# One kernel, four edits: the scan's block matrix built by overlapping reads from DRAM, the modulation split over two stages, and weights loaded in another order

## What is computed

```python
def reference(x, c, ...):
    cond = jax.nn.silu(c)
    for i in range(DEPTH):
        mod = cond @ ada_w[i] + ada_b[i]
        sh1, sc1, g1, sh2, sc2, g2 = jnp.split(mod, 6, axis=-1)
        hn = modulate(rmsnorm(x, norm1_g[i]), sh1, sc1)
        ...  # out = s5_mixer(hn, ...) in layer 0, short_conv_mixer in layer 1
        x = x + (1 + g1)[:, None, :] * out
        hn = modulate(rmsnorm(x, norm2_g[i]), sh2, sc2)
        x = x + (1 + g2)[:, None, :] * hier_moe(hn, ...)
    return rmsnorm(x, final_g)

def s5_mixer(h, w_in, ...):
    u = (h @ w_in).astype(f32)
    ...  # st[t] = a * st[t-1] + b u[t] for each group, in chunks
    ...  # y = Re(c st) + d_skip * u
    val, gate = jnp.split(gelu(y) @ w_glu, 2, axis=-1)
    return val * jax.nn.sigmoid(gate)
```

## Time and profile before

| | us |
|---|---|
| median of 3 runs | 7016.55 (7015.04 to 7017.35) |
| the profiled execution | 7015.28 |
| its span | 7013.7 |
| PE busy | 6407.3 (91%) |
| DVE busy | 3326.9 (47%) |
| ACT busy | 2051.1 (29%) |
| POOL busy | 1448.3 (21%) |

### The profile page before, as it was taken

The page is one execution under the profiler, slowest core; times in us unless marked ns, Lnnn a source line. Parts: engine busy times, 40 slices in busy tenths (PEclk is TensorE's granted clock), DMA queues, the critical chain, the costliest instruction groups (busy, mean ns, idle before and its releaser), DMA issues. The chain is left out here.

```text
span 7013.7 us, 90561 instructions
## 1 busy us (share of the span) xinstructions
PE 6407.3 (91%) x30729; PEld 5236.7 (75%) x30730; DVE 3326.9 (47%) x4885; ACT 2051.1 (29%) x3301; POOL 1448.3 (21%) x1250
## 2 busy tenths in 40 slices
PE   6997888799996999999997999998998699999994
PEld 1876667588884788888886888886776588888883
DVE  4445666343336555555643422222545654466554
ACT  1112443222221343343433500000111243344434
POOL 0001222488002232222321000000000322232222
PEclk8998999899998999999998999999998899999997
DMA  6221111444222676676754544433334365677766
GB/s 205 66 87 46 48 50 48 158 142 144 85 84 79 199 223 178 186 215 200 225 157 149 194 178 166 148 135 137 133 131 141 117 189 167 191 217 237 222 200 244
DMA packets 528270, 1073.08 MB, mean 153 GB/s; under 512 B 59550, under 2 KB 137374, under 8 KB 527146
## 3 DMA queue, kind: packets, MB, share of 16 engines
q1 hardware_dynamic: 425364, 805.88, 33.6%
q0 software_dynamic: 69888, 249.12, 14.1%
q10 hardware_dynamic: 32920, 16.80, 0.8%
HBM read 816.33 MB, written 255.38 MB: 153 GB/s over the span
## 5 line engine op out<-in xcount | busy, mean ns | idle before, releaser
L127 PE MATMUL conv_p<-conv_x_lo,conv_w_hi 128*128 128x512 f32 x1536 | 601.1, 391 | 0.0
L128 PE MATMUL conv_p<-conv_x_hi,conv_w_lo 128*128 128x512 f32 x1536 | 598.5, 390 | 0.0
L129 PE MATMUL conv_p<-conv_x_hi,conv_w_hi 128*128 128x512 f32 x1536 | 598.3, 390 | 0.0
L1758 DVE SCALAR_TENSOR_TENSOR m_o<-m_pO,m_weight_of,m_gate 128x512 f32<-128x512 f32 x320 | 237.0, 746 | 726.6 <-POOLq L1398 376.6
L1725 DVE TENSOR_TENSOR m_w_lo<-m_w_raw,m_w_hi 128x1024 fp32r<-128x1024 f32 x496 | 577.6, 1214 | 0.0
L1533 ACT ACTIVATE m_xT_hi<-m_pX 128x512 fp32r<-128x512 f32 x320 | 191.6, 599 | 1151.9 <-PE m_pB L129 994.2
L127 PE MATMUL m_pA<-m_w_lo,m_xT_hi 128*128 128x512 f32 x1280 | 517.0, 404 | 5.7 <-DVE m_xT_lo L1736 5.7
L1474 PE MATMUL m_pO<-m_w_lo,m_hT_hi 128*128 128x512 f32 x1280 | 512.8, 401 | 0.5 <-ACT m_hT_hi L1538 0.5
L1521 ACT ACTIVATE m_w_hi<-m_w_raw 128x1024 fp32r<-128x1024 f32 x512 | 505.3, 1053 | 0.0
L129 PE MATMUL m_pA<-m_w_hi,m_xT_hi 128*128 128x512 f32 x1280 | 503.0, 393 | 0.0
L128 PE MATMUL m_pA<-m_w_hi,m_xT_lo 128*128 128x512 f32 x1280 | 499.9, 391 | 0.0
(11 more groups left out here) (354 smaller groups left out, 12702.6 us busy)
## 6 DMA issues: line engine op xcount, KB each, us to landing
m_w_raw<-in_moe_w_dram SPq DMA_DIRECT2D x384, 1024.0 KB, 7.3
conv_x_hi<-hT_hi SPq DMA_DIRECT2D x24, 2048.0 KB, 9.3
conv_x_lo<-hT_lo SPq DMA_DIRECT2D x24, 2048.0 KB, 13.9
mod_w<-in_ada_w_dram SPq DMA_DIRECT2D x12, 2048.0 KB, 7.8
glu_ada<-in_ada_w_dram POOLq DMA_DIRECT2D x96, 256.0 KB, 3.1
a_x<-in_x_dram SPq DMA_DIRECT2D x32, 512.0 KB, 3.5
u<-a_stage POOLq DMA_DIRECT2D x4, 4096.0 KB, 19.2
s_u<-u SPq DMA_DIRECT2D x64, 256.0 KB, 2.6
```

Source lines behind the costliest of these rows:

```text
L127: pe.matmul(out, lh, rl, start=start, stop=False)
L128: pe.matmul(out, ll, rh, start=False, stop=False)
L129: return pe.matmul(out, lh, rh, start=False, stop=stop)
L1758: dve.scalar_tensor_tensor(out=ob[:, n, :], in0=pO[:, n, :], scalar=wslot[:, bass.ds(tile_, 1)], in1=gate2[:, n, :], op0=ALU.mult, op1=ALU ...
```

## The change

1. **Tables.** `Modulation` computes only 4 of the 12 chunks (`sh1`, `sc1`), with a buffer for each; SP issues them after the small loads. Its first loads go out on ACT, and POOL adds the biases and stores the row. `skip` is loaded by four DMAs on POOL into four blocks of 16 partitions; DVE and PE no longer wait for it.
2. **Input.** The other 8 chunks are summed on POOL (`PartialSums`, the code that "glu" had, with three slots in place of four), two chunks ahead of each of the four stores of `u`. After the last tile SP reads the partial sums (2 MB), PE adds up their partitions in eight products, ACT copies them and stores them to `mod`. The three constants are issued by POOL, `w` is loaded and split in pieces of 256 rows by 512 columns, bank by bank, and the times in a block are stored in reverse.
3. **Scan.** The four groups of a batch share one PSUM bank `pK`: each group adds one product of `z[g]` (its b in 16 of 128 columns) with `O`. Once a batch `out_k` adds the skip and copies it out; SP stores it to DRAM behind a pad of zeros, waits, and loads `R` of each group by a read whose eight row blocks overlap, each 16 elements further. `inside` waits for these loads.
4. **Projection.** `src` goes out first, then the weights in pieces by bank (1 MB in "glu", 0.5 MB in "cout"). POOL issues the eight constants when the sixth piece has landed, and DVE folds them after the weights are split.

```diff
     def loads(self, sp):
-        with sp.Fori(1, self.ROUNDS) as i:
-            self.load(sp, i, 0)
-            self.load(sp, i, 1)
-
-    def store(self, sp):
-        sp.wait_ge(self.added, 2 * self.ROUNDS)
-        sp.dma_start(self.dst, self.row[:]).then_inc(self.st, 16)
-        sp.wait_ge(self.st, 16)
+        for q in range(self.CHUNKS):
+            sp.dma_start(self.w[q][:], self.w_view[:, :, bass.ts(q, HALF)]).then_inc(self.w_ld[q], 16)
...
+    def products(self, pe):
         pe.wait_ge(self.cond_ready, 1)
-
-    def products(self, pe, a, b):
-
-        with pe.Fori(a, b) as i:
-            for s in range(2):
-                pe.wait_ge(self.w_ld[s], 16 * i + 16)
-                pe.wait_ge(self.out[s], i + 1)
-                for k in range(KD):
-                    last = pe.matmul(self.ps[s][0:1, :], self.cond_sb[:, 1, k:k + 1], self.w[s][:, k, :],
-                                     start=k == 0, stop=k == KD - 1)
-                last.then_inc(self.mm[s], 1)
+        for q in range(self.CHUNKS):
+            pe.wait_ge(self.w_ld[q], 16)
+            if q >= 2:
+                pe.wait_ge(self.out, q - 1)
+            for k in range(KD):
+                last = pe.matmul(self.ps[q % 2][0:1, :], self.cond_sb[:, 1, k:k + 1], self.w[q][:, k, :],
+                                 start=k == 0, stop=k == KD - 1)
+            last.then_inc(self.mm, 1)
...
+    def biases(self, pool):
+        pool.wait_ge(self.b_ld, 16)
+        for q in range(self.CHUNKS):
+            pool.wait_ge(self.out, q + 1)
+            c = bass.ts(q, HALF)
+            pool.tensor_tensor(self.row[0:1, c], self.row[0:1, c], self.bias[0:1, c], ALU.add).then_inc(self.added, 1)
+        pool.wait_ge(self.added, self.CHUNKS)
+        pool.dma_start(self.dst, self.row[:]).then_inc(self.st, 16)
+        pool.wait_ge(self.st, 16)
...
+    def run(self, pool, first, end):
+        for n in range(first * KD, end * KD):
+            q, k, s = n // KD, n % KD, n % self.SLOTS
+            pool.wait_ge(self.ld[s], 16 * (n // self.SLOTS) + 16)
+            if k == 0:
+                pool.wait_ge(self.bias, 16 * q + 16)
+                if q >= 1:
+                    pool.wait_ge(self.st, 16 * q)
+            pool.tensor_scalar(self.buf[s][:], self.buf[s][:], self.cond[:, 1, k:k + 1], None, ALU.mult).then_inc(self.step, 1)
+            pool.wait_ge(self.step, 2 * n + 2)
+            pool.tensor_tensor(self.acc[:], self.buf[s][:], self.zero[:] if k == 0 else self.acc[:], ALU.add) \
+                .then_inc(self.step, 1)
+            pool.wait_ge(self.step, 2 * n + 3)
+            if n + self.SLOTS < self.chunks * KD:
+                self.load(pool, n + self.SLOTS)
+            if k == 0 and q + 1 < self.chunks:
+                self.load_bias(pool, q + 1)
+            if k == KD - 1:
+                pool.dma_start(self.out[q], self.acc[:]).then_inc(self.st, 16)
...
+            sp.wait_ge(part_ready, 1)
+            for s in range(2):
+                sp.wait_ge(mm[s], 2 + NT)
+            sp.dma_start(part.rearrange("p (q n) -> p q n", n=HALF), partial[0:PARTS].rearrange("q p n -> p q n")).then_inc(p_ld, 16)
...
+            pool.dma_start(gain[:], row(norm_g[0:1, :], 0, D)).then_inc(const_ld, 16)
+            load_mod(pool, mod_dram, 0, SC1, scale[:], const_ld)
+            load_mod(pool, mod_dram, 0, SH1, shift[:], const_ld)
+            pool.memset(ones[:], 1.0).then_inc(ones_set, 1)
+            later.clear(pool)
+            later.start(pool)
             pool.sem_inc(stage_free, 1)
-            with pool.Fori(0, NT // BLK) as n:
+            for n in range(NT // BLK):
+                later.run(pool, PARTS * n // (NT // BLK), PARTS * (n + 1) // (NT // BLK))
                 pool.wait_ge(blk_ready, BLK * n + BLK)
-                pool.dma_start(u_view[bass.ds(n, 1)].squeeze(0), stage[:]).then_inc(blk_stored, 16)
-                pool.wait_ge(blk_stored, 16 * n + 16)
-                pool.sem_inc(stage_free, 1)
+                pool.dma_start(u_view[n], stage[:]).then_inc(blk_stored, 16)
+                if n + 1 < NT // BLK:
+                    pool.wait_ge(blk_stored, 16 * n + 16)
+                    pool.sem_inc(stage_free, 1)
+            later.finish(pool)
+            pool.sem_inc(part_ready, 1)
+            pool.wait_ge(blk_stored, 16 * (NT // BLK))
...
+            pe.wait_ge(ones_set, 1)
+            pe.wait_ge(p_ld, 16)
+            for q in range(PARTS):
+                if q >= 4:
+                    pe.wait_ge(p_out, q - 3)
+                pe.matmul(sum_of(q), ones[:], part[:, q * HALF:(q + 1) * HALF], start=True, stop=True).then_inc(p_mm, 1)
...
+            for q in range(PARTS):
+                act.wait_ge(p_mm, q + 1)
+                act.activation(part_out[:, q * HALF:(q + 1) * HALF], sum_of(q), ACT.Copy).then_inc(p_out, 1)
+            act.wait_ge(p_out, PARTS)
+            act.dma_start(mod_dram[0:1, FIRST:], part_out).then_inc(p_st, 16)
+            act.wait_ge(p_st, 16)
...
-            for i in range(SB):
-                get(tab.skip[i * CH:(i + 1) * CH, :], d_skip[0].rearrange("(g c) -> c g", c=CH), True)
             mod.loads(sp)
-            mod.store(sp)
...
+            def toeplitz(i, s):
+
+                b = 2 * i + s
+                sp.wait_ge(k_out, b + 1)
+                sp.dma_start(k_dram[s][:, PAD:], ks[s][:]).then_inc(k_st[s], 16)
+                sp.wait_ge(k_st[s], 16 * i + 16)
+                for g in range(BG):
+                    moved = bass.AP(tensor=k_dram.tensor, offset=(s * P + g * LANES) * (PAD + L * CH),
+                                    ap=[[CH, SB], [PAD + L * CH, CH], [1, L * CH]])
+                    sp.dma_start(flat(R[s][g][:]), moved).then_inc(r_ld[s], 16)
+
+            sp.wait_ge(zeroed, BG + 2)
+            for s in range(2):
+                sp.dma_start(k_dram[s][:, 0:PAD], pad[:]).then_inc(pad_st[s], 16)
+            load(0, 0, (0, 1))
+            def body(i, first, last):
+                for s in range(2):
+                    load(i, s, (2, 3))
+                    if not (last and s == 1):
+                        load(*at(i, s, 1), (0, 1))
+                    toeplitz(i, s)
+            pairs(sp, NB // 2, body)
...
+            for g in range(BG):
+                pool.memset(z[g][:], 0.0).then_inc(zeroed, 1)
+            pool.memset(diag[:], 0.0).then_inc(zeroed, 1)
+            pool.memset(pad[:], 0.0).then_inc(zeroed, 1)
...
-                c(dve.tensor_single_scalar(z[q][:, SB - 1, :], tab.b1[:, gs, :].squeeze(1), 1.0, ALU.mult))
+                dve.tensor_single_scalar(z[g][:, g * LANES:g * LANES + CH], tab.b1[:, gs, :].squeeze(1), 1.0, ALU.mult) \
+                   .then_inc(b_ready, 1)
...
-            def out_r(i, s, g):
-                n = number(i, s, g)
-                dve.wait_ge(r_psum, n + 1)
-                r = flat(R[s][g][:])
-                dve.scalar_tensor_tensor(out=r[:, 0:P], in0=ident[:], scalar=tab.skip[:, bass.ds(n, 1)],
-                                         in1=flat(pR[:])[:, 0:P], op0=ALU.mult, op1=ALU.add)
-                dve.tensor_copy(r[:, P:], flat(pR[:])[:, P:]).then_inc(r_out, 1)
+            def out_k(i, s):
+                b = 2 * i + s
+                dve.wait_ge(k_psum, b + 1)
+                dve.wait_ge(k_st[s], 16 * i)
+                dve.scalar_tensor_tensor(out=ks[s][:, 0:CH], in0=diag[:], scalar=tab.skip[:, bass.ds(b, 1)],
+                                         in1=pK[:, 0:CH], op0=ALU.mult, op1=ALU.add)
+                dve.tensor_copy(ks[s][:, CH:], pK[:, CH:]).then_inc(k_out, 1)
...
-                pe.wait_ge(r_out, n + 1)
+                pe.wait_ge(b_ready, n + 1)
                 pe.wait_ge(tab_o, n + 1)
-                o, r = flat(O[s][g][:]), flat(pR[:])
-                for j in range(SB):
-                    pe.matmul(r[:, j * CH:P], flat(z[q][:])[:, (SB - 1 - j) * CH:(SB - 1 - j) * CH + P],
-                              o[:, 0:(SB - j) * CH], start=j == 0, stop=False, skip_group_check=True)
-                pe.matmul(r[:, P:], flat(pt[q][:])[:, (KB - 1) * P:], o[:, CH:CH + (KB - 1) * P],
-                          start=False, stop=True, skip_group_check=True).then_inc(r_psum, 1)
+                if g == 0:
+                    pe.wait_ge(k_out, 2 * i + s)
+                last = pe.matmul(pK[:], z[g][:], flat(O[s][g][:])[:, 0:L * CH], start=g == 0, stop=g == BG - 1)
+                if g == BG - 1:
+                    last.then_inc(k_psum, 1)
...
-                pe.wait_ge(r_out, n + 2)
+                if g == 0:
+                    pe.wait_ge(r_ld[s], 16 * BG * (i + 1))
...
+        KQ = NB_
+
+        def piece(w, q):
+
+            b, k = order[q * KQ // KD], q * KQ % KD
...
+            for q in range(KD):
+                sp.dma_start(piece(w_raw, q), piece(w.rearrange("(k p) n -> p k n", p=P), q)).then_inc(w_ld[q], 16)
+                if q == 1:
+                    load_x(0, 0)
...
+            pool.wait_ge(w_ld[KD - 3], 16)
+            constants_of(pool)
...
```

(9 more changed lines are left out.)

275 lines of the change are left out of this document (129 added, 146 removed).

## The result

The changed kernel takes **6900.2 us** (median; 6899.0 to 6904.2) where the kernel before takes 7015.8 (four runs): a ratio of 0.9837, 95% interval 0.9821 to 0.9852. The forecast was 6865, so 35 us of the expected gain did not come.

| term (forecast) | before | after | difference |
|---|---|---|---|
| tables, to the next phase's first load (-56) | 134.23 | 84.88 | -49.4 |
| input stage to its last product (0 of the +8) | 428.0 | 441.4 | +13.4 |
| tail after it (+8) | 19.4 | 26.3 | +6.8 |
| scan, start to first `s_before`, the first batch included (-2, and 4.5 of the -67) | 73.3 | 65.6 | -7.7 |
| scan, the other 14 periods of `s_before` (63 of the -67) | 600.9 | 543.7 | -57.2 |

The account below looks back on a forecast made before the run. Each stage was taken as bound by its own last wait, the scan by TensorE and VectorE together. -56 + 8 - 2 - 67 - 29 - 6 = -152 from 7015.28 gave 6865 us, range 6830 to 6905.

Parts of the forecast that it names:

- Part 1: Tables: loads leave VectorE's path, its chain ends at 78, the next phase starts at 78.5: -56 us, bounds -42 and -62.
- The load case: Tables: `skip` and two `mod_w` loads both leave the wait, VectorE starts at 24.0; 34 if only `skip` counts.
- VectorE's chain keeps its 54 us: Tables: VectorE's own work stays 54 us long, ends at 78 and is last in the stage.
- Part 2: Input stage: POOL's steps hidden beside TensorE, head 0, longer tail for partial sums: +8 us, bounds +4 and +18.
- at the head ... I take 0: Input stage's start: competing row broadcasts 0 to +3, new piece order 0 to -2, taken together as 0.
- Part 3: Scan's start: SP's waits +2.5, prologue without VectorE's waits -8, late third `u` load +3.5: -2 us, bounds -6 and +4.
- Part 4: Scan's batches: TensorE and VectorE lose work per group, 4.5 us a batch times 15: -67 us, bounds -30 and -95.
- The step from 5.2 to 4.5: Scan: gain per batch is 5.2 us without VectorE's collisions with POOL, 4.1 followed through with them; 4.5 taken.
- Part 5: Glu stage's head: earlier `src` and weight pieces end tile 0 31 sooner, constants give 2 back: -29 us, bounds -18 and -33.
- Part 6: Conv projection's head: same reordering with two banks, limited by late constants: -6 us, bounds -12 and 0.
- VectorE and POOL exclude each other throughout: Rival, chance 0.12: in the scan four instructions lose 0.77 us each, so -32 in place of -67: 6900.
- The clock drops more often: Rival, chance 0.12: in the scan every batch pays 2.8 us, and half as much again for deeper drops: 6895.

Follow-up runs that it names:

- The bias product: Changed kernel with the tables' modulation bias added by a ninth TensorE product instead of by GpSimd, which only stores the row: 6893.5 us.

## Why the prediction was right, and where 35 us went

The time lies inside the range, 5 us from its upper end, and that is in part luck. The sum allowed for independent errors of about 30. But Parts 1, 2, 4, 5 and 6 all missed on the slow side, Part 2 beyond its own bound of +18, and about half of the loss has one cause, GpSimd's instructions beside VectorE's (4 us in the tables, 8.5 in the head, about 6 in the scan).

**Part 1, forecast -56, measured -49.4.** The load case was right: VectorE starts at 25.95 where I had 24.0. The step that failed is "VectorE's chain keeps its 54 us": it took 57.9, because four bias additions were moved to GpSimd beside it. I had looked at what the additions would cost as the last link, not at what they do to the engine that is last. The bias product shows it.

**Part 2, +8, measured +20.2.** The tail was sized well: the partial sums landed 13.8 us after TensorE's last product (forecast 14), and eight products took 9.0 (forecast 10). The read goes out 0.02 us behind a 4 MB store and is served beside it: it lands 12.1 us after its issue, and 8.1 when it is alone; first come, first served would have put it behind the store's 19. The Trainium skill (DMA: Bandwidth & Descriptors, Queues, rings and completion order) says that each DMA engine takes turns between queues; the trace agrees, by these numbers. The step that failed is "at the head ... I take 0", with +3 as its bound: it cost 12.2. POOL's steps I had called "hidden" because they lie beside TensorE, but at the head TensorE waits for VectorE. 8.5 of the 12.2 are GpSimd's instructions, 1.9 the constants' queue, and 1.8 stay open.

**Part 3, -2, measured -7.7 with the first batch in it.** That batch's 4.5 belong to Part 4, so the forecast for this row is -6.5. From the phase's start to TensorE's first scan level it is 35.6 us, before 40.8: -5.2, where my -8 and SP's +2.5 make -5.5 (TensorE's first transposes start 1.4 us later). From there to `s_before` it is 30.0, before 32.5: -2.5, with 1.96 us of waiting behind the first trip, for which I had 3.5.

**Part 4, -67, measured -57 without the first batch.** TensorE's work fell by 36.3 - 30.1 = 6.2 us a batch, my 6.3. For the 14 periods of the table the forecast is 14 x 4.5 = 63; the period after them, 24.7 us, prepares nothing and did not change. The step from 5.2 to 4.5, "the two `table_p` instructions cost about 0.7 more", is mis-sized: beside GpSimd they take 0.33 and 0.77 longer, 1.1 for group 2. For group 3 it is 0.5, as its product already met GpSimd before, which I had not counted. I had read the price off one sum in the earlier trace rows. The rest is the clock. VectorE's product of group 3 before, and the windows of two batches before:

```profile
937.45 1.32 DVE L703 TENSOR_TENSOR s_pt<-bc,pow_back 128x512 f32 x1
```
```profile
913.89:955.02 41.13, 36.28 (x232) 28.79 (x232) 27.11 (x60) 17.14 (x44) 8.86 (x8) 1.00 0.09 26
955.02:998.95 43.93, 37.97 (x232) 30.44 (x232) 26.69 (x60) 17.14 (x45) 8.87 (x8) 0.96 0.23 72
```

The 4.1 that came is a mean of unlike things: a shorter batch went from 41.1 to 38.5, 2.6 only; a longer one from about 44 to 39.6. In the shorter one TensorE's busy time fell by 4.4 (36.3 to 31.9), 1.7 less than at full clock, and the time in which it isn't busy grew by 1.8. Before, every second batch had its clock fall; after, every batch has a little of it (0.96 and 0.91).

**Part 5, -29, measured -24.9.** TensorE has tile 0 done 35.3 us after the phase's start (forecast 36), though two weight pieces came 1.5 us late. What was too small is the 2 us that the constants give back. The fold comes at 36.5 (forecast 34), and `low` for tile 1 behind it; TensorE waits 4.5 us for it and then, up to 1262, runs at a clock of 0.83. PE:

```profile
1244.69 1.94 PE L1272 MATMUL glu_pT<-ident,glu_src 128*128 128x128 f32 x8 [4.50 <-DVE glu_sT_lo L1153]
```

**Part 6, -6, measured 0.** The mechanism I gave limits more than I allowed. VectorE, then PE:

```profile
4784.83 1.22 DVE L287 SCALAR_TENSOR_TENSOR cout_gain<-cout_hn,cout_gain 128x1024 f32<-128x1024 f32 x1 [7.26 <-DMA cout_router_bias<-in_moe_be_dram]
4786.82 1.23 DVE L1153 TENSOR_TENSOR cout_sT_lo<-cout_src,cout_sT_hi 128x1024 fp32r<-128x1024 f32 x1
4788.10 0.80 PE L127 MATMUL cout_pM<-cout_w_lo,cout_sT_hi 128*128 128x512 f32 x1 [6.82 <-DVE cout_sT_lo L1153]
```

The constants are issued 15.5 us after the start (forecast 12.5) and the fold is 27.4 in, so `low` for tile 1 ends at 30.6 where I had tile 1 start at 27.5. TensorE has tile 0 done 23.8 us after the start, some 10 earlier than before, and gives all of it back: it waits 6.8 us for that `low` and does tile 1 at a clock of 0.80.

**The rivals.** "VectorE and POOL exclude each other throughout" named 6900, and the kernel takes 6900, but not by its arithmetic: it put its 35 us all into the scan, where 6 are (63 forecast for the 14 periods, 57 measured); 16 are in VectorE's chain of the tables (3.9) and in the head (12.2), where no rival looked. That its number came out is chance. Its mechanism is right and was priced too low: taking GpSimd out of VectorE's way is worth 4.0, 8.5 and 54 us in the three stages. The Trainium skill (SBUF — State Buffer, Who interferes with whom) describes an exclusion for VectorE instructions with two SBUF inputs, and says that copies and `tensor_scalar`, which have one, can enter modes with two ports and then contend too. The two-input rows agree (1.28 and 0.22 us). `s_z` is a `tensor_scalar` with one SBUF input and was held as well, 0.94 and 0.17; which mode it ran in no trace here shows. I had read that rule only for the stage where a row of before showed a slow instruction. "The clock drops more often" was part of the truth, as effect and not as cause: TensorE's busy time in the 14 periods has some 25 us of it, where before seven batches had 1.7 each. The trip of `R` is hidden, as forecast, but for 2 us in the first batch.

## What to carry to other kernels

Work given to an idle GpSimd is not free because TensorE is busy: ask what VectorE does at that moment, and whether anyone waits for it. If VectorE is the late one, move GpSimd's operations into VectorE's idle time with more buffers; taking single VectorE instructions out from beside them won 0.3 us a batch at most. When batches alternate between two lengths, forecast the undisturbed one and the clock's part apart, and don't put the whole difference down to the clock. A load that an engine issues behind a wait is hidden in a full pipeline and may not be in the first round.

## What the runs showed of the hardware that I had not expected

- A GpSimd addition on one partition (1 x 512, 1.26 us) holds a VectorE instruction on 128 partitions for its whole length: 0.22 became 1.28 us.
- Operations with one small SBUF input are held too: a 128 x 16 scaling 0.94 for 0.17 us, a 16 x 16 copy 1.0 for 0.16 us. A VectorE copy out of PSUM is not: `s_p` (128 x 512) took 0.69 us in all 64 groups, and in 62 of them it ran beside GpSimd's terms.
- GpSimd pays as well: `s_t2o` took 1.53 us beside VectorE and 1.08 alone.
- Three row broadcasts issued from POOL's queue, with `x` and 4 MB of weights on SP's, were in 12.4 to 12.7 us after the phase's first load in the ten kernels that issue them there, with or without 0.75 MB of other loads behind them; issued first on SP's queue, 8.8.
